# Pooled branches beside the last attention steps: by token chunk and alternating groups, the fourth chunk between the divisions

## The reference

```
u = rms_norm(h, norm_mix[l])
proj = u @ w_in[l]
q, k, v, z, g_att, g_pool = jnp.split(proj, ...)
q = partial_rope(...); k = partial_rope(...)
att = dilated_attention(...)                 # (B, S, 512), combined over the 3 groups
pooled = multiscale_pool(z)                  # trailing mean over 2, 4, 8, 16 tokens, minus the token
pooled = einsum(pooled, w_pool_group[l]) * pool_scale[l]
merged = sigmoid(g_att) * (att @ w_att_branch[l]) + sigmoid(g_pool) * (pooled @ w_pool_branch[l])
h = h + merged @ w_out[l]
```

## Time and profile before

| what | value |
|---|---|
| median of the runs | 1221.65 us (lowest 1219.14) |
| profiled execution | 1221.88 us; span of its slowest core, core 3, 1220.3 us |
| spans of the 8 cores | 1212.2 to 1220.3 us |
| mean granted TensorE clock of core 3 | 0.987 |
| PE busy, share of the span | 1158.0 us, 95% |
| DVE, ACT busy | 574.6 us (47%), 439.7 us (36%) |
| chain that ended last, by engine | PE 87%, DVE 6%, DMA 3%, ACT 2%, issue 2% |

### The profile page before, as it was taken

How to read it: one execution, slowest core, us unless ns; L and a number is a source line. 1 busy time by engine, 2 the same in 40 slices (tenths; PEclk the granted TensorE clock), 3 DMA queues, 4 the chain that set the end, 5 groups by cost and what they waited for, 6 DMA issues and landing times.

```text
span 1220.3 us, 21261 instructions; the slowest of 8 cores (1212.2 to 1220.3 us)
## 1 busy us (share of the span) xinstructions
PE 1158.0 (95%) x8292; PEld 643.4 (53%) x8292; DVE 574.6 (47%) x867; ACT 439.7 (36%) x710; POOL 68.8 (6%) x134
## 2 busy tenths in 40 slices
PE   3888899999999999799999999999999999999997
PEld 2454766576686666344444444444444444444476
DVE  3346566755654558874444466412213232112455
ACT  3464555745654564572222132311120032111211
POOL 0001000000001010100111100000000000000000
PEclk9899899999999999999999999999999999999999
DMA  8847633233324321212554512244602813446722
GB/s 198 235 112 207 137 79 75 47 83 73 75 50 86 80 48 40 53 22 62 127 150 98 82 31 48 57 78 90 117 18 51 148 35 70 83 78 107 164 105 104
DMA packets 32706, 109.96 MB, mean 90 GB/s; under 512 B 4704, under 2 KB 11104, under 8 KB 26720
## 3 DMA queue, kind: packets, MB, share of 16 engines
q0 software_dynamic: 15264, 69.76, 30.3%
q1 hardware_dynamic: 17344, 38.84, 10.8%
HBM read 148.31 MB, written 16.06 MB: 135 GB/s over the span
## 4 chain that ended last, share of the span: by engine, by line
PE 87%; DVE 6%; DMA 3%; ACT 2%; issue 2%; SPq 0%; DVEq 0%; POOL 0%; ACTq 0%; POOLq 0%
PE ps_p L197 50%; PE ps_s L197 17%; PE ps_o L197 16%; PE ps_o L200 3%; DVE uto L210 1%; DMA xs<-x 1%; DMA rin<-qk 1%; DVE ta L207 1%; ACT rs L204 1%; DMA qk<-rout 1%; DVE rt L207 1%; DVE acc L207 1%; DVE uth L210 0%; DMA rps<-rin 0%; DMA rout<-rp 0%
## 5 line engine op out<-in xcount | busy, mean ns | idle before, releaser
L197 PE MATMUL ps_p<-uto,wp 128*128 128x512 bf16 (+1 forms) x784 | 182.4, 385 | 15.4 <-DVE uto L210 11.0
L197 PE MATMUL ps_o<-ftv,wguv 128*128 128x512 bf16 x640 | 144.7, 379 | 0.0
L197 PE MATMUL ps_s<-ftv,wguv 128*128 128x512 bf16 x640 | 144.7, 379 | 0.0
L197 PEld LDWEIGHTS ps_p<-uto,wp 128*128 128x128 bf16 x784 | 76.0, 100 | 107.7 <-issue 27.1
L197 PE MATMUL ps_p<-actt,wdv 128*128 128x512 bf16 (+1 forms) x616 | 115.2, 349 | 2.0 <-DVE actt L207 2.0
L204 ACT ACTIVATE qk<-ps_p 128x512 bf16<-128x512 f32 (+2 forms) x122 | 69.8, 577 | 107.8 <-PE ps_p L197 94.5
L207 DVE TENSOR_TENSOR acc<-ps_o,acc 128x1024 f32<-128x1024 f32 x32 | 65.1, 2034 | 84.3 <-PE ps_s L197 51.1
L197 PEld LDWEIGHTS ps_s<-ftv,wguv 128*128 128x128 bf16 x640 | 62.6, 98 | 75.5
L197 PEld LDWEIGHTS ps_o<-ftv,wguv 128*128 128x128 bf16 x640 | 62.6, 98 | 75.5
L197 PE MATMUL ps_p<-wp,uto 128*128 128x128 bf16 x1536 | 98.7, 226 | 0.8 <-ACT qk L204 0.8
L197 PEld LDWEIGHTS ps_p<-wp,uto 128*128 128x128 bf16 x1536 | 96.0, 122 | 6.5 <-issue 1.8
(11 more groups left out here) (118 smaller groups left out, 1427.8 us busy)
## 6 DMA issues: line engine op xcount, KB each, us to landing
wguv<-wgu POOLq DMA_DIRECT2D x20, 1024.0 KB, 7.7
wp<-w_in POOLq DMA_DIRECT2D x12, 768.0 KB, 7.6
wdv<-wd POOLq DMA_DIRECT2D x6, 1408.0 KB, 19.2
ht<-x SPq DMA_DIRECT2D x32, 256.0 KB, 4.7
xs<-x SPq DMA_DIRECT2D x3, 2048.0 KB, 16.5
xs<-x POOLq DMA_DIRECT2D x3, 2048.0 KB, 10.4
xs<-x SPq DMA_DIRECT2D x4, 1024.0 KB, 17.8
oT<-ost SPq DMA_DIRECT2D x12, 256.0 KB, 2.4
```

Of the source, the lines that this page charges most:

```text
L197: return P.op("pe", lambda e: e.matmul(out, lhsT=lhsT, rhs=rhs, start=start, stop=stop), after)
```

## The change

The order of the work from the fifth projection item of unit 11 on is written anew.

- `iters` starts with (0,0), (1,0), (0,1), (1,1), (0,2), (0,3), (1,2), (1,3) in place of output chunk 0 and then 1. So the second pair of gate items already uses ring slot 1.
- The z items come by token chunk, groups alternating, for chunks 0 to 2. Chunk 3 of the four groups is issued after the attention, one item behind each division, its `pooled` one item later and its `pool_mm` in iterations 3 and 4.
- The tiles `pre[i]` go round by a counter, and `t_pl` is kept per chunk, so that a `yp_item` waits for the maps of its own chunk.
- The distance of unit 10's steps is 2 or 3 items in place of 3, that of unit 11's 1 or 2 in place of 1. Before the gate items 4 to 7 the steps of unit 10 are brought to their end.
- yp items 0 to 3 stand between the last steps; the loads for output chunks 2 and 3 move behind the iterations that free their slots.
- `sigl` tiles lie elsewhere and wait for what lay there before.

```
@@ since[0], need[0] @@
-            since[0], need[0] = 0, 1 + s % 2 if even[0] is None else even[0]
+            since[0], need[0] = 0, 1 + s % 2 if even[0] is None else even[0] + s % 2
@@ pooled @@
-        i = tg
+        i = npre[0] % 4
+        npre[0] += 1
@@ pool_mm @@
+        t_pl[tg].append(bank_free[k])
@@ iters, sigl @@
-            for o in (6320, 3168, 2112, 1056, 0, 4224, MERGED + 2048, MERGED + 3072)]
+            for o in (6320, RP, MERGED + 2048, MERGED + 3072, RP + 1024, A0 + 8864, A0 + 9888, A0 + 10912)]
-    iters = [(dc, tg) for dc in range(8) for tg in range(4)]
+    iters = [(0, 0), (1, 0), (0, 1), (1, 1), (0, 2), (0, 3), (1, 2), (1, 3)]
+    iters += [(dc, tg) for dc in range(2, 8) for tg in range(4)]
@@ yp_item @@
-                       after=[t_pb[dc], t_pl[0], bank_free[k]])
+                       after=[t_pb[dc], bank_free[k]] + t_pl[tg])
@@ the mix @@
-    mix = [x_ for k in range(4) for x_ in (own[4 + k], z[k])] + [x_ for k in range(4) for x_ in (vown[k], z[4 + k])]
-    mix += [x_ for k in range(4) for x_ in (g[k], z[8 + k])] + [x_ for k in range(3) for x_ in (z[12 + k], g[4 + k])] + [z[15]]
-    even[0] = 3
+    mix = [own[4], z[3][0], own[5], own[6], z[2][0], own[7], vown[0], z[1][0], vown[1], g[0], z[3][1], g[1], vown[2], z[2][1],
+           vown[3], z[1][1], z[0][0], g[2], z[0][1], g[3], z[3][2], g[4], z[2][2], g[5], z[1][2], g[6], z[0][2], g[7]]
+    even[0] = 2
...
+    for item in mix:
+        if item in g[4:8]:
+            while pend[0][0] <= 10:
+                do_step()
+        mixed(item, 11 if item is own[7] else None)
...
-        if k == 18:
-            finish_turns()
+        if t_rope[11] and not ring1:
             load_gates(1, [t_rope[11]])
             load_ab(1, [])
             load_pb(1, [])
+            ring1 = True
         if steps and steps[0][0] == 11:
-            even[0] = 0
-    left = [g[7]]
+            even[0] = None
+    left = yp[0:4]
...
@@ after the attention @@
     finish(*norm_q.pop(0))
+    mixed(z[3][3])
     finish(*norm_q.pop(0))
-    for item in g[8:10]:
-        item(later)
+    mixed(z[2][3])
     for it in range(32):
+        if 4 <= it < 8:
+            yp[it]()
...
         if it < 2:
             finish(*norm_q.pop(0))
-            g[10 + it](later)
+            mixed(z[1 - it][3])
         if it == 2:
-            for tanh, k, ps, t in later:
-                tanh(k, ps, t)
+            pooled(*late.pop(0))
+            for item in g[8:14]:
+                item()
+            load_gates(2, pe_now())
         if it == 3:
-            g[12]()
-            g[13]()
-            gates(8)()
+            pool_mm()
+            pool_mm()
         if it == 4:
             g[14]()
             g[15]()
             load_gates(3, pe_now())
+            while b1_pend:
+                pool_mm()
         if it == 5:
+            load_ab(2, pe_now())
+            load_pb(2, [])
...
         if it == 23:
-            P.wait("pool", t_b1)
+            P.wait("pool", all_toks())
```

More of the change, by code:

```diff
@@ L738, in _body @@
     b1_pend = []
-    t_pl = [None]
+    t_pl = [[] for _ in range(4)]
+    npre = [0]
     t_wlast = [None]
@@ L759, in pooled @@
         zb_free[gz][tg % 2] = tab_last[0] = t_p
-        b1_pend.append((gz, i, slice(tg * 512, tg * 512 + 512), t_p))
+        b1_pend.append((gz, i, tg, t_p))
     def z_item(gz, tg):
@@ L780, in pool_mm @@
     def pool_mm():
-        gz, i, cols, t_p = b1_pend.pop(0)
+        gz, i, tg, t_p = b1_pend.pop(0)
+        cols = slice(tg * 512, tg * 512 + 512)
         k, psp = take_bank()
@@ L784, in pool_mm @@
                          after=[t_p, t_wpg, bank_free[k]])
-        t_pl[0] = bank_free[k] = act(poolt[gz][:, cols], psp[:], AF.Copy,
-                                     after=[pre_free[i], slot_free[0], t_wlast[0] if gz == 0 else None],
-                                     scale=cstv[:, 24 + gz:25 + gz])
+        bank_free[k] = act(poolt[gz][:, cols], psp[:], AF.Copy,
+                             after=[pre_free[i], slot_free[0], t_wlast[0] if gz == 0 else None],
+                             scale=cstv[:, 24 + gz:25 + gz])
+        t_pl[tg].append(bank_free[k])
     merged = bf("merged_", MERGED, 8 * 2048).rearrange("p (c t) -> p c t", c=8)
@@ L836, in tanh @@
         def tanh(k, ps, t):
-            free = [None] if it == 0 else zb_free[4 - it] if it < 5 else [tab_last[0]] if it == 5 else [slot_free[1]]
-            t_sig[it][h] = bank_free[k] = act(sigl[it][h], ps[:], AF.Tanh, after=[t] + list(free), scale=0.5)
+            free = None if it == 0 else rope_free[0] if it in (1, 4) else slot_free[1] if it < 4 else slot_free[2]
+            t_sig[it][h] = bank_free[k] = act(sigl[it][h], ps[:], AF.Tanh, after=[t, free], scale=0.5)
         return emit
@@ L862, in _body, with mixed @@
     retire(9)
-    z = [z_item(gz, tg) for gz in (3, 2, 1, 0) for tg in range(4)]
+    z = [[z_item(gz, tg) for tg in range(4)] for gz in range(4)]
     g = [gate_item(n) for n in range(16)]
-    yp = [yp_item(it, None if it < 6 else it - 4) for it in range(8)]
-    mix = [x_ for k in range(4) for x_ in (own[4 + k], z[k])] + [x_ for k in range(4) for x_ in (vown[k], z[4 + k])]
-    mix += [x_ for k in range(4) for x_ in (g[k], z[8 + k])] + [x_ for k in range(3) for x_ in (z[12 + k], g[4 + k])] + [z[15]]
-    even[0] = 3
-    for k, item in enumerate(mix):
+    yp = [yp_item(it) for it in range(8)]
+    mix = [own[4], z[3][0], own[5], own[6], z[2][0], own[7], vown[0], z[1][0], vown[1], g[0], z[3][1], g[1], vown[2], z[2][1],
+           vown[3], z[1][1], z[0][0], g[2], z[0][1], g[3], z[3][2], g[4], z[2][2], g[5], z[1][2], g[6], z[0][2], g[7]]
+    even[0] = 2
+    def mixed(item, u_done=None):
         prev = late.pop(0) if late else None
-        run(item, 11 if item is own[7] else None)
+        run(item, u_done)
         if prev:
             pooled(*prev)
+    ring1 = False
+    for item in mix:
[3 more added lines that the diff above has]
+        mixed(item, 11 if item is own[7] else None)
         if item is vown[3]:
             t_wlast[0] = pe_now()[0]
-        if k == 18:
-            finish_turns()
+        if t_rope[11] and not ring1:
             load_gates(1, [t_rope[11]])
@@ L880, in _body @@
             load_pb(1, [])
+            ring1 = True
         if steps and steps[0][0] == 11:
-            even[0] = 0
-    left = [g[7]]
+            even[0] = None
+    left = yp[0:4]
     while late:
-        run(left.pop(0))
         pooled(*late.pop(0))
-    while b1_pend or steps:
-        if steps:
-            do_step()
+    while steps:
+        do_step()
         if b1_pend:
@@ L893, in _body @@
             left.pop(0)()
+    while pend:
+        weighted(pend.pop(0))
+    due[0] = False
+    while b1_pend:
+        pool_mm()
     for item in left:
         item()
[L896 to L901, removed]
     def all_toks():
         return [Tok(P.esem[e], P.ecnt[e]) for e in P.CE]
-    t_b1 = all_toks()
     ht = [f32("ht_", (UT_H + c * 2048) if c < 4 else HT4 if c == 4 else HT5 + 2048 * (c - 5), 2048) for c in range(8)]
@@ L968, in _body @@
     finish(*norm_q.pop(0))
+    mixed(z[3][3])
     finish(*norm_q.pop(0))
-    for item in g[8:10]:
-        item(later)
+    mixed(z[2][3])
     for it in range(32):
+        if 4 <= it < 8:
+            yp[it]()
         if it < 8:
-            if it >= 4:
-                yp[it]()
             light(it)
@@ L992, in _body @@
             load_gates(3, pe_now())
+            while b1_pend:
+                pool_mm()
         if it == 5:
+            load_ab(2, pe_now())
+            load_pb(2, [])
+        if it == 6:
+            gates(8)()
+        if it == 7:
+            load_ab(3, pe_now())
+            load_pb(3, [])
             pfree[1] = list(bank_free)
             gates(9)()
-        if it == 7:
-            pfree[1][2:4] = bank_free[2:4]
-            load_pb(3, pe_now())
         if 8 <= it < 30:
@@ L1002, in _body @@
             load_gates((it + 2) // 4 + 2, pe_now())
-        if it % 4 == 3 and it < 24:
+        if it % 4 == 3 and 8 < it < 24:
             load_ab(it // 4 + 2, pe_now())
-            if it > 8:
-                load_pb(it // 4 + 2, [])
+            load_pb(it // 4 + 2, [])
         if it == 7:
```

## The result

The changed kernel takes 1235.37 us in the median, the kernel before took 1221.2 beside it: the ratio is 1.0115, with a 95% interval of 1.0102 to 1.0129. That is 14 us slower: clear of the noise, and less than the 2% that count as a difference.

The page of the kernel after, engine totals and the chain that ended last.

A forecast was written before the change was run, and what follows sets the result against it. PE was taken as the bound, its idle time as the prize. Gate opening 503.2, dense work (118.1 - 45.2), clock 3.1 and later waits 8.4 give a stage end of 587.6, 12.5 us later: 1234.4, range 1226 to 1241.

The forecast's parts named there:

- The alternation removes the holes of 480 to 510: Stretch 480 to 510: a group's buffers are used far apart, ACT's halo copy needn't wait for DVE; gain at most 14.9 us.
- PE gets to gate item 2 at 487.2: From 442.05, 45.4 us of queued work less 0.2 bring PE to ga_103 at 487.2, with no hole.
- DVE's last turn ends at 488.8: From 457.5 DVE's queue takes 30.8 us plus half a microsecond until the rotation's last turn ends; 1.5 us either way.
- The chain takes 14.4 us: On POOL's queue, write, read-back and loads of ga and gp after the last turn take 14.4 us; gate opens at 503.2.
- The wait is 16.0 us: PE idles 16.0 us at gate item 2, from 487.2 until slot 1's weights are there at 503.2.
- The rule of the Trainium skill on the shared port: POOL's DMAs can starve beside DVE: last three each up to 2.5 us earlier, sum 1227; the forecast went by the rows.
- The clock costs 3.1: PE's granted clock falls behind the gate wait: 3.1 us of work lost after the restart, bounds 0 and 3.8.
- The six later waits are 8.4 us: PE waits: 0.9 adjacent steps, 1.5 and 1.4 acc, 1.4 first division, 1.7 light item 2, 1.5 yp item 5; together 8.4.
- At nothing: Later loads for chunks 2 and 3, POOL's wait at iteration 23, deferred z items: no cost; uncovered loads up to 5 us each.
- (a): Gate opens at 501.5, clock doesn't fall, later waits sum to 4: stage ends at 578.4, time 1225; chance 0.13.
- (c): After the gate wait the clock stays at half until the divisions, some 40 us costing 20, not 3.1: 1251; chance 0.04.
- (b): Gate item 2's weights are there when PE comes: stage ends at 568.6, 6.5 us less, time 1215.4; chance 0.05.

The follow-up runs named there:

- the run with the copy: Kernel after, with gate items 2 and 3 reading a second copy of slot 1's weights loaded at the stage's start: 1220.86 us, ratio 0.9999.
- the run with copy and earlier turn: Kernel after, with the copied slot 1 weights and group 3's second z item moved behind the v items: 1220.50 us, ratio 0.9995.
- the filled wait: Kernel after, with 72 matmuls without use ahead of gate item 2: 1232.56 us, ratio 1.0097.
- two ways to have the weights in time: Kernel after with copied slot 1 weights and earlier turn, 1220.50 us; or slot 0 for gate items 2 and 3, earlier turn, slot 1 loads before the read-back, 1220.79.
- the run on the halo copy: Kernel with copied weights and earlier turn, with group 0's first-chunk item moved ahead of the other three groups' items: 1217.43 us, ratio 0.9970.
- the last run: Kernel with new iteration order, earlier turn, early load and reordered tail: group 0's first-chunk item moved first, z[2][2] and g[4] swapped; 1215.04 us, ratio 0.9949.
- the run before it: Kernel with copied weights, earlier turn and group 0's first-chunk item first, with z[2][2] and g[4] swapped besides: median 1220.13 us, ratio 0.9984.

## Why the prediction was right, step by step

The time was 1.0 us over the forecast; the stage itself took 1.6 us more (147.15 in place of 145.55). The steps can be followed one by one. Predicted times are shifted by 1.05 us here, since the stage starts at 441.00 on the profiled core and started at 442.05 before.

- *The alternation removes the holes of 480 to 510.* True as far as it can be seen: none is listed ahead of the gate item but 0.58 us at the stage's start. But the claim that ACT's halo copy no longer waits for DVE holds in the kernel after only because everything waits longer elsewhere. With the weights in time the copy of group 0's second chunk waited 2.98 us in the run with the copy and 4.76 in that with copy and earlier turn. That step was wrong, and the gate wait hid it.
- *PE gets to gate item 2 at 487.2*, shifted 486.15; it was 502.49 - 16.21 = 486.28.
- *DVE's last turn ends at 488.8*, shifted 487.75; it was 487.51. The first turn, said to start at 475 (shifted 473.95), started at 473.71. That the end is right to a quarter of a microsecond is in part luck: the queue's first addition to acc started at 456.87, 0.4 us behind the forecast (456.45, shifted), and from there the queue took 30.6 us in place of 31.3. Half a microsecond of that is group 1's tile: the price of 3.3 us, from the earlier trace rows, has an idle time of 0.46 in it, and the tile took 2.8 here.
- *The chain takes 14.4 us*; it took 14.8: the read-back landed later, and gp in 4.8 in place of 4.6.
- *The wait is 16.0 us*; it was 16.21. The copy, which takes this wait and the clock behind it out, brought back the whole loss.
- *The rule of the Trainium skill on the shared port* (SBUF — State Buffer, section "SBUF: two separate sides") would, as the prediction read it, have had the last DMAs land faster with DVE idle, and by that estimate the sum was 1227. The reading was wrong. In that section of the Trainium skill the rule is tied to DVE operations in a mode that uses two ports, and `tensor_tensor` is said to have no such mode. Most of DVE's operations ahead of these DMAs are TENSOR_TENSOR, so no run here tests the rule. What the rows show is that DVE's work made no difference: gp took 4.8 us to land with DVE busy 0.17 of the 5 us around its issue, where it took 4.6 and 4.7 beside a busier DVE.
- *The clock costs 3.1*; the filled wait measured 2.8, and the lines behind the wait give 2.7. The row it was taken from the earlier trace rows was a little dearer.
- *The six later waits are 8.4 us.* They were 0.78, 1.68, 1.49, 1.55, 1.71 and 1.56, 8.8 together, each at the place and with the releaser that was named. The term that was mis-sized is the conversion of a hole to lost time: 0.16 us for each hole was counted in the kernel before and left out for the six new ones, 1.0 us.
- The sum by measured terms: 61.3 us until the gate opens (502.3 - 441.0), 0.2 until PE starts, 72.9 of dense work, 2.7 of clock, 8.8 of holes and 1.0 for their starts are 146.9 of 147.15 us.
- *At nothing:* no load of chunks 2 and 3 is waited for; the only DMA in the list of PE's waits in the stage is gp.

Of the rivals, (a) did not come: the gate opened at 502.3, and the clock fell. Nor did (c): the eight matmuls at 508.81, 6.3 us behind the restart, took 1.89 us again. Its limit was added up wrong, besides: 24.4 us for 2% less the 12.5 of the forecast, plus the 3.1 of clock already in it, are 15.0 us of lost work, so 30 us at half clock and not 26. Rival (b), weights in time and 1215.4, could be tried, and its price was wrong by 5 us: two ways to have the weights in time gave 1220.5 and 1220.8. It assumed that PE then meets only the 8.4 us, because my account of DVE stopped at the last turn. Going on, it would have shown four pooled tiles ahead of the first mask and the first addition. The wait for the DMA covered this backlog, and whoever takes the wait away gets it in its place. Some 1215 are reached only after the halo copy, the tail and the order of DVE's work have been changed as well, and then DVE sets the end of the stretch.

## What to carry to other kernels

When a ring of buffers is used in a new order, ask of each first use which queue loads it and what stands ahead of that load; here one swapped pair of iterations put a chain of three DMAs, 14.8 us, ahead of the last projections. When a wait is to be removed, carry the account of the next slowest engine past it, because the wait hides that engine's backlog: of 18.9 us of wait and clock 14.5 came back here with a copy of 512 KB, and each further microsecond had to be taken from DVE's and ACT's order. Where an engine copies a few columns for later, look at what is queued behind the copy: 0.22 us of work held an Exp, and with it PE, for over 3 us.

## What the runs showed of the hardware

Behind 16.2 us of waiting 2.7 us of work were lost to the clock's fall. Behind 3.58 us, in the run with copy and earlier turn, the eight matmuls of 1.89 us took 3.60, about as long as the 3.57 behind the long wait, and with the lines around them some 2.6 us were lost. Between these two the length of the wait did not set the price. It was lower, about 1.3 us, behind the 2.58 us in the run on the halo copy (four lines of 1.01, 0.61, 0.61 and 1.52 us in place of 0.61, 0.40, 0.39 and 1.03).

What makes it fall was less regular. Waits of 0.78 us left it at 1.00; in the last run waits of 1.18, 1.93 and 1.40 us within 12 us left it at 1.00 (505 to 525), while 1.60 and 2.02 us within 6 us, in the run before it, are followed by lines at half speed (1.01 us for eight short matmuls in place of 0.61). In the run with the copy alone the eight matmuls right behind 2.54 us still took 0.40, and only the next eight, after 0.76 us more of waiting, took 0.61. So short holes are cheap until one is not, and one that is a little longer may cost one to three microseconds more.
